# First head pair projected inside the scan's output projection, gate tiles shifted by two units

## What is computed

```python
h = rms_norm(x, g); proj = h @ w_in          # z, xbc, dt, q_a, kv_a, k_rope, gates
y_ssd = ssd_mixer(z, xbc, dt, ...) @ w_ssd_proj                # 2048 -> 1024
q  = (rms_norm(q_a) @ w_uq).reshape(16 heads, 96); kv = rms_norm(kv_a) @ w_ukv
q, k = rope(rms_norm(q)), rope(rms_norm(concat(k_nope, k_rope)))
y_mla = causal_attention(q, k, v) @ w_mla_proj
g_ssd, g_mla = split(sigmoid(gates + gate_b))
x = x + (g_ssd * y_ssd + g_mla * y_mla) @ w_o    # then a gated feed-forward part
```

## Time and profile before

| | us |
|---|---|
| median of three runs | 1760.62 (1758.84 to 1761.57) |
| the profiled execution | 1760.32 |
| its span | 1758.5 |
| TensorE, VectorE, ScalarE, GpSimd busy | 1672.8, 1079.1, 813.1, 629.1 |
| mean granted TensorE clock | 0.983 of 2.4 GHz |

### The profile page before, as it was taken

The page is one execution under the profiler, slowest core; times in us unless marked ns, Lnnn a source line. Parts: engine busy times, 40 slices in busy tenths (PEclk is TensorE's granted clock), DMA queues, the critical chain, the costliest instruction groups (busy, mean ns, idle before and its releaser), DMA issues.

```text
span 1758.5 us, 22676 instructions
## 1 busy us (share of the span) xinstructions
PE 1672.8 (95%) x7960; PEld 1316.0 (75%) x7979; DVE 1079.1 (61%) x1659; ACT 813.1 (46%) x1344; POOL 629.1 (36%) x275
## 2 busy tenths in 40 slices
PE   7999899999999799999999999999989999999999
PEld 5688677767787588766667877777768788888887
DVE  6599377666526677677778237777746555556200
ACT  5423366655334355466655235655543344444210
POOL 4244211232444144344434532222224244444442
PEclk9999899999999899999999999999999999999999
DMA  6233221121433223211112321111123233333331
GB/s 204 64 96 96 78 67 48 60 72 48 149 103 96 91 84 107 73 49 48 39 47 72 108 80 47 55 49 51 59 88 104 73 96 97 97 98 100 98 96 60
DMA packets 40119, 142.72 MB, mean 81 GB/s; under 512 B 4696, under 2 KB 5176, under 8 KB 39648
## 3 DMA queue, kind: packets, MB, share of 16 engines
q1 hardware_dynamic: 37600, 131.96, 24.6%
q10 hardware_dynamic: 2432, 9.59, 1.6%
HBM read 137.31 MB, written 4.21 MB: 80 GB/s over the span
## 4 chain that ended last, share of the span: by engine, by line
PE 78%; DVE 12%; ACT 6%; issue 3%; POOL 0%; ACTq 0%; DVEq 0%; POOLq 0%
PE bank L693 16%; PE bank L695 15%; PE bank L694 15%; PE bank L1274 4%; PE bank L1275 4%; PE bank L1273 4%; PE bank L1178 1%; PE bank L744 1%; PE bank L746 1%; PE bank L745 1%; PE bank L834 1%; PE bank L1089 1%; PE bank L1199 1%; PE bank L852 1%; PE bank L1187 1%
## 5 line engine op out<-in xcount | busy, mean ns | idle before, releaser
L584 POOL TENSOR_TENSOR w_lo<-w_raw,w_hi 128x1024 fp32r<-128x1024 f32 x243 | 591.5, 2436 | 1090.8 <-ACT w_hi L1295 946.5
L693 PE MATMUL bank<-u_hi,w_hi 128*128 128x512 f32 x776 | 326.8, 421 | 19.5 <-DVE taps L2269 10.6
L1295 ACT ACTIVATE w_hi<-w_raw 128x1024 fp32r<-128x1024 f32 x199 | 209.1, 1055 | 222.2 <-PE bank L695 177.0
L695 PE MATMUL bank<-u_hi,w_lo 128*128 128x512 f32 x776 | 305.0, 393 | 0.0
L694 PE MATMUL bank<-u_lo,w_hi 128*128 128x512 f32 x776 | 304.7, 393 | 0.0
L693 PEld LDWEIGHTS bank<-u_hi,w_hi 128*128 128x128 f32 x776 | 147.4, 190 | 78.4 <-issue 30.1
L695 PEld LDWEIGHTS bank<-u_hi,w_lo 128*128 128x128 f32 x776 | 146.8, 189 | 32.2
L694 PEld LDWEIGHTS bank<-u_lo,w_hi 128*128 128x128 f32 x776 | 147.6, 190 | 29.4 <-issue 3.4
L1273 PE MATMUL bank<-u_hi,w_hi 128*128 128x512 f32 x320 | 124.5, 389 | 0.0
L1274 PE MATMUL bank<-u_lo,w_hi 128*128 128x512 f32 x320 | 124.5, 389 | 0.0
L1275 PE MATMUL bank<-u_hi,w_lo 128*128 128x512 f32 x320 | 124.5, 389 | 0.0
(11 more groups left out here) (461 smaller groups left out, 3583.9 us busy)
## 6 DMA issues: line engine op xcount, KB each, us to landing
w_raw<-weights SPq DMA_DIRECT2D x243, 512.0 KB, 3.5
xt<-x_t SPq DMA_DIRECT2D x8, 256.0 KB, 6.6
hank<-bias_dram ACTq DMA_DIRECT2D x8, 256.0 KB, 3.1
xt<-x_t ACTq DMA_DIRECT2D x1, 2048.0 KB, 9.2
h_dram<-h_res ACTq DMA_DIRECT2D x1, 2048.0 KB, 7.0
h_res<-h_dram ACTq DMA_DIRECT2D x1, 2048.0 KB, 7.8
out<-h_res SPq DMA_DIRECT2D x8, 256.0 KB
p_val<-p_t ACTq DMA_DIRECT2D x1, 512.0 KB, 11.3
```

The costliest lines, as they stand in the source:

```text
L584: pool.tensor_tensor(w_lo[:, j, :], w_raw[:, j, :], w_hi[:, j, :].bitcast(F32), ALU.subtract).then_inc(w_lo_ready, 1)
L693: pe.matmul(o, hi, xh, start=(i == 0), stop=False)
L695: mm = pe.matmul(o, lo, xh, start=False, stop=(i == n - 1))
L1295: act.activation(w_hi[:, c % RING, :], w_raw[:, c % RING, :], ACT.Copy).then_inc(w_hi_ready, 1)
```

## The change

Seven of the eight `ssd_out` tiles turn over banks 0 and 3; the eighth lies in bank 3 and is cut into parts (0, 4), (4, 10) and (10, 16), with the keys, both queries and the sums of the first pair between. The sums of the rope part move to bank 7, and their square goes to `sq_q` ahead of ScalarE's read of the first tile. Of the first gate tile four units stand at the entry instead of eight. So in each pair a gate tile ends at steps 1 and 5 instead of 3 and 7, and the last pair has twelve units instead of eight. `key_spread` stands behind the gate units of step 4. On ScalarE the tanh comes at steps 2 and 6, the roots come ahead of the exponential of step 3, and weights are split at steps 2 and 6 instead of 0, 2 and 4. In the last pair four of the eight `o_hi` and `o_lo` are made at steps 3 to 7. `q_s`, `k_s`, `probs_x` and `turned_x` change places, and `o_hi` and `o_lo` become eight tiles each. The load of `h_res` is issued before the last sum is awaited.

```diff
@@ -147,8 +147,8 @@
-    plan.use_banks(0, 1, 2, 3)
-    plan.columns("ssd_out", 8, 16, "A")
+    plan.use_banks(0, 3)
+    plan.columns("ssd_out", 7, 16, "A")
@@ -162,23 +162,30 @@
+    plan.use_banks(3)
+    parts = [(c, s) for c in (plan.chunk(), plan.chunk()) for s in range(CH)]
+    t = plan.open("ssd_out", parts, [])
...
+    query(1, c)
+    plan.fill(t, "A")
...
-    query(1, c)
-    plan.fill(mix_gate(0, plan.chunk()), "A")
+    t = mix_gate(0, plan.chunk())
...
-        if h + 1 < XH:
+        more = h + 1 < XH
+        if more:
...
-        t = mix_gate(h, plan.chunk())
-        if h + 1 < XH:
+        gates = [plan.chunk() for _ in range(1 + more)]
+        if more:
...
+        plan.fill(t, "A")
+        if more:
...
-        plan.fill(t, "A")
-        if h + 1 < XH:
-            plan.fill(mix_gate(h + 1, plan.chunk()), "A")
+        plan.fill(mix_gate(h, gates[0]), "A")
+        if more:
+            t = mix_gate(h + 1, gates[1])
@@ -436,11 +443,11 @@
-        probs_x = at("probs_x", 56, [P, 4, S])
-        turned_x = at("turned_x", 64, [P, 4, S])
+        probs_x = at("probs_x", 186, [P, 4, S])
+        turned_x = at("turned_x", 194, [P, 4, S])
...
-        q_s = at("q_s", 186, [P, 4, S])
-        k_s = at("k_s", 194, [P, 4, S])
+        q_s = at("q_s", 56, [P, 4, S])
+        k_s = at("k_s", 64, [P, 4, S])
@@ -454,8 +461,8 @@
-        o_hi = at("o_hi", 186, [P, KD, S], F32R)
-        o_lo = at("o_lo", 104, [P, KD, S], F32R)
+        o_hi = [at(f"o_hi{i}", kb, [P, S], F32R) for i, kb in enumerate((166, 168, 202, 204, 186, 188, 190, 192))]
+        o_lo = [at(f"o_lo{i}", kb, [P, S], F32R) for i, kb in enumerate((136, 138, 140, 142, 144, 146, 148, 194))]
@@ -1100,7 +1107,7 @@
-            for i, t in enumerate(st["ssd_out"]):
+            for i, t in enumerate(st["ssd_out"][0:7]):
@@ -1128,9 +1135,8 @@
-                pe.wait_ge(act_freed, st["ssd_out"][7]["freed"][1])
...
-                    mm = pe.matmul(bank[3][:, ti:ti + 1], probs_x[NOPE:QK, 3, ti * P:(ti + 1) * P],
+                    mm = pe.matmul(bank[7][:, ti:ti + 1], sq_q[NOPE:QK, ti * P:(ti + 1) * P],
@@ -1204,26 +1210,34 @@
-            gate0 = st["mix_gate"][0]
+            gate0, last_out = st["mix_gate"][0], st["ssd_out"][7]
+            def of_y(k):
+                return y_hi[:, k, :], y_lo[:, k, :]
+            rope_sums()
...
+            column_tile(last_out, of_y, part=(0, 4))
+            project_query(1)
+            query_sums(0)
+            column_tile(last_out, of_y, part=(4, 10))
+            key_sums(0)
+            query_sums(1)
+            column_tile(last_out, of_y, part=(10, 16))
+            key_spread(0)
...
-            column_tile(gate0, of_u2, part=(0, 2))
-            rope_sums()
-            query_sums(0)
-            key_sums(0)
+            column_tile(gate0, of_u2, part=(0, 1))
...
-            project_query(1)
-            column_tile(gate0, of_u2, part=(2, 5))
-            query_sums(1)
-            column_tile(gate0, of_u2, part=(5, 7))
-            key_spread(0)
+            column_tile(gate0, of_u2, part=(1, 3))
+            pe.wait_ge(act_freed, last_out["freed"][1])
+            head_logits(0)
...
-            column_tile(gate0, of_u2, part=(7, 8))
-            for n in range(3):
-                head_logits(n)
+            head_logits(1)
+            head_logits(2)
+            column_tile(gate0, of_u2, part=(3, 4))
@@ -1233,12 +1247,13 @@
+                g, k = divmod(16 * p + 2 * i + 4, KD)
+                if more or i < 4:
+                    column_tile(st["mix_gate"][g], of_u2, part=(k, k + 2))
+                else:
+                    column_tile(st["mix_gate"][XH - 1], of_u2, part=(i, i + 1))
...
-                if more:
-                    column_tile(st["mix_gate"][2 * p + 1 + i // 4], of_u2, part=(i % 4 * 2, i % 4 * 2 + 2))
-                else:
-                    column_tile(st["mix_gate"][2 * p + 1], of_u2, part=(i, i + 1))
@@ -1251,7 +1266,7 @@
-            column_tiles(st["mla_out"], lambda k: (o_hi[:, k, :], o_lo[:, k, :]), n_lo["o"] - KD, pair=True)
+            column_tiles(st["mla_out"], lambda k: (o_hi[k][:, :], o_lo[k][:, :]), n_lo["o"] - KD, pair=True)
@@ -1724,17 +1739,19 @@
-            for i, t in enumerate(st["ssd_out"]):
-                for c, s in t["parts"][:-1]:
-                    if s == CH - 1:
-                        split_weights(c)
+            act.wait_ge(lo_ready, n_lo["kn"])
+            act.activation(sq_q[NOPE:QK, :], small2[NOPE:QK, :], ACT.Square).then_inc(krope_sq, 1)
+            def scan_out(i):
+                t = st["ssd_out"][i]
...
-            act.wait_ge(h_spilled, 16)
-            act.activation(probs_x[NOPE:QK, 3, :], small2[NOPE:QK, :], ACT.Square).then_inc(krope_sq, 1)
+            for i in range(7):
+                split_weights(st["ssd_out"][i]["parts"][0][0])
+                scan_out(i)
@@ -1788,28 +1805,29 @@
+            act.wait_ge(krope_summed, 1)
...
-            act.wait_ge(krope_sq, 1)
...
+            query_squares(1)
+            split_weights(st["ssd_out"][7]["parts"][0][0])
+            act.wait_ge(krope_added, 1)
+            head_norms(0)
+            scan_out(7)
...
-            query_squares(1)
-            after(st["head_q"][1])
-            act.wait_ge(krope_added, 1)
-            head_norms(0)
...
-            mix_gate(0)
-            after(st["mix_gate"][0])
...
-                if p and i == 0:
+                if i == 2:
...
-                if more and i == 4:
+                if more and i == 6:
...
+                if more and i == 3:
+                    head_norms(p + 1)
@@ -1817,21 +1835,19 @@
-                if more and i == 3:
-                    head_norms(p + 1)
...
-                if p and i == 0:
-                    after(st["mix_gate"][2 * p])
-                if more and i == 2:
-                    after(st["head_q"][2 * p + 3])
-                if more and i == 4:
+                if i == 2:
+                    after(st["head_q"][2 * p + 3] if more else st["mix_gate"][2 * p])
+                if more and i == 6:
...
+                if not more and 3 <= i < 7:
+                    act.wait_ge(k_ready, XH)
+                    act.activation(o_hi[i - 3][:, :], o_raw[:, i - 3, :], ACT.Copy).then_inc(hi_ready, 1)
+            act.dma_start(h_res[:, :, :].rearrange("p a b -> p (a b)"), h_dram).then_inc(h_back, 16)
+            for i in range(4, KD - 1):
+                act.activation(o_hi[i][:, :], o_raw[:, i, :], ACT.Copy).then_inc(hi_ready, 1)
...
-            act.dma_start(h_res[:, :, :].rearrange("p a b -> p (a b)"), h_dram).then_inc(h_back, 16)
-            for i in range(KD - 1):
-                act.wait_ge(x_out, i + 1)
-                act.activation(o_hi[:, i, :], o_raw[:, i, :], ACT.Copy).then_inc(hi_ready, 1)
-            act.activation(o_hi[:, KD - 1, :], bank[7][:, :], ACT.Copy).then_inc(hi_ready, 1)
+            act.activation(o_hi[KD - 1][:, :], bank[7][:, :], ACT.Copy).then_inc(hi_ready, 1)
@@ -2467,6 +2483,7 @@
+            dve.wait_ge(h_spilled, 16)
@@ -2474,22 +2491,22 @@
-            query_features(0, 0)
-            key_features(0)
-            query_features(0, 1)
...
-            values_out(0)
...
-            dve.tensor_scalar(krope_bias[:, :], bank[3][:, 0:NT], 1.0 / QK, EPS, ALU.mult, ALU.add).then_inc(krope_added, 1)
-            values_out(1)
+            dve.tensor_scalar(krope_bias[:, :], bank[7][:, 0:NT], 1.0 / QK, EPS, ALU.mult, ALU.add).then_inc(krope_added, 1)
+            query_features(0, 0)
+            key_features(0)
+            query_features(0, 1)
...
+            values_out(0)
+            values_out(1)
@@ -2519,13 +2536,15 @@
-                if i == 6 and 2 * p + 1 < KD:
+                if i == 7 and 2 * p + 1 < KD:
...
+                if not more and 4 <= i < 8:
+                    low(o_raw[:, i - 4, :], o_hi[i - 4][:, :], o_lo[i - 4][:, :])
...
+            for i in range(4, KD - 1):
+                low(o_raw[:, i, :], o_hi[i][:, :], o_lo[i][:, :])
...
-            for i in range(KD - 1):
-                low(o_raw[:, i, :], o_hi[:, i, :], o_lo[:, i, :])
-            low(bank[7][:, :], o_hi[:, KD - 1, :], o_lo[:, KD - 1, :])
+            low(bank[7][:, :], o_hi[KD - 1][:, :], o_lo[KD - 1][:, :])
```

## The result

The changed kernel takes 1776.13 us (median; 1775.17 to 1777.97), the kernel before in the same comparison 1759.74 us (1758.84 to 1761.57). The ratio is 1.0093, 95% interval 1.0076 to 1.0111: the change makes the kernel 16.4 us slower. The profiled execution has a span of 1776.2 us, 17.7 above that of before, and a mean clock of 0.977 (0.983 before).

What follows compares the result with a forecast made beforehand. TensorE, busy for 95% of the span, was taken to bound the kernel. The terms 10.3 + 2.0 - 2.7 + 4.2 - 0.5 - 4.8 = +8.5 us on 1760.32 gave 1769 us, range 1758 to 1778.

Steps and rivals of the forecast that it cites:

- rival A: The whole sum as it stands: 1769 us, own range 1764 to 1774; chance 0.55.
- rival E: A second table load at the tanh of step 6, or like collisions: 9.0 us more, 1777.8; chance 0.14.
- Part 1: Scan's output projection: TensorE waits for a bank until ScalarE reads tile 0, +10.3 us; half clock behind it, +2.0 us.
- Rival D: Banks cost nothing if ScalarE drains tile 0 before the latents: 1756.5 us, faster; chance 0.05.
- Part 2: Entry into the attention: old idle and half clock go, three new gaps and one half-clock stretch come; -2.7 us.
- three gaps: Entry waits: second query for its bank 2.0 us, second half of values 0.9, fourth logits block behind a table load 1.1.
- term of the clock: Entry: one half-clock stretch behind the first gap, chance about a half, counted as 1.5 us.
- Part 3: Seven pairs with a successor: old waits go, waits for tanh and turned_x come; +0.6 us each, +4.2 together.
- Rival B: Pairs come out even, one wait replaced by another: 1764.6 us; chance 0.18.
- Rival C: Pairs lose all waits and gain 11.8 us, the tanh off TensorE's path: 1752.8 us; chance 0.08.
- Part 4: Last pair: a wait of 0.95 goes, 0.42 comes, -0.5 us; exit: shorter wait and less half clock, -4.8 us.

Runs made afterwards that it cites:

- one part alone: Kernel before, with only the scan's eight output tiles turning over banks 0 and 3: 1771.3 us beside 1760.7, ratio 1.0063.
- banks-back version: Changed kernel, with the scan's first seven output tiles turning over banks 0, 1, 2, 3, 0, 3, 0: 1759.94 us, ratio 0.9995.
- last version: Combined version, with the tanh of each pair's odd gate tile one step earlier on ScalarE: 1747.25 us, ratio 0.9920.
- combined version: Banks-back version, with the wait for the second query filled, second weight copy two steps later, key spread ahead of step 4's gate units: 1751.9 us, ratio 0.9954.
- experiment at the exit: Banks-back version, with the four result tiles split during the last pair split behind it instead: 1762.21 us, ratio 1.0010.
- version with the copy moved: Banks-back version, with ScalarE's second weight copy of step 2 moved to step 4 in each pair: 1755.35 us, ratio 0.9973.
- changed kernel with the filled gap: Changed kernel, with seven units instead of four of the last scan tile ahead of the second head's query: 1771.99 us, ratio 1.0055.

## Why the prediction was right, and where it was not

The forecast was 1769 us, slower, in a range of 1758 to 1778; the time is 1776.13. The sign and the main mechanism were right, the size was short: 8.5 us were forecast, 16.4 measured. That the time still lies in the range is in part luck: it is above 1774, where the range of the sum itself (rival A) ended, and what stretched the range upwards was rival E, whose mechanism did not come. The same execution, step by step, from the table of starts:

**Part 1, the banks.** Forecast +10.3 and +2.0 us, measured +10.3 and +1.7. The first 7 tiles end 13.5 us later, of which 1.5 lie ahead of the wait, in stages that the change does not touch. The forecast's start of 973.8 for the waiting matmul is 975.32 with that 1.5. Shown by one part alone (10.5 us slower) and by undoing it (16.2 us faster). Rival D, that the banks cost nothing, is out.

**Part 2, the entry.** Forecast -2.7, measured about -0.2. From the end of the seventh tile to the keys of the second round it takes 2.1 us less; 2.7 of gate work have left this stretch for the last pair, and one longer pair (0.86) lies in it. The three gaps came as told: 1.88 (forecast 2.0), 0.90 (0.9), 0.92 (1.1). The step that failed is the term of the clock: I counted 1.5 us lost, and 3.2 were lost. That it comes with the bank wait I had not seen at all; I had priced both waits by themselves.

**Part 3, the pairs.** Forecast +0.6 us a pair, measured +0.86: 31.6 us from keys to keys instead of 30.75. The waits at the tanh of step 2 (listed 0.24; forecast 0.42) and for `turned_x` (0.77; 0.8) came; in the three pairs with half clock 0.46 and 0.60 for the keys take the place of the latter. In a pair at full clock four waits sum to 1.61 us, where two of 1.38 were before. The other 0.63 us are busy time (30.01 against 29.38), and the starts tell what it is. Timeline of the changed kernel, the same small matmul without and with a wait behind it:

```profile
1138.86 0.22 PE L1185 MATMUL bank<-tri_b,squares_b 128*128 128x128 bf16 x1
1138.89 0.48 PE L700 MATMUL bank<-u_hi,w_hi 128*128 128x512 f32 x1
...
1143.32 0.22 PE L1185 MATMUL bank<-tri_b,squares_b 128*128 128x128 bf16 x1
1143.78 0.50 PE L700 MATMUL bank<-u_hi,w_hi 128*128 128x512 f32 x1 [0.24 <-ACT gm L1785]
```

The next matmul starts 0.03 us later in the one case and 0.46 in the other: a wait listed with 0.24 us costs 0.43, as forecast from starts. So a listed wait is short by about 0.2 us, and four small waits cost more than two with nearly the same sum.

The step that failed in the pairs is one that the sum did not have: three of the seven have half clock in their middle, and such a pair takes 32.96 us. Keys of three rounds in the changed kernel (timeline), 32.96 and 31.63 us apart:

```profile
1100.38 0.47 PE L1131 MATMUL bank<-kn_hi,w_hi 128*128 128x512 f32 x1
...
1133.34 0.47 PE L1131 MATMUL bank<-kn_hi,w_hi 128*128 128x512 f32 x1
...
1164.97 0.47 PE L1131 MATMUL bank<-kn_hi,w_hi 128*128 128x512 f32 x1
```

That is 3 x 1.35 = 4.1 us, and with 7 x 0.86 the pairs cost 10.1 us and not 4.2. Rival B (pairs even) is half right in the runs: the banks-back version is level with the kernel before, but because the exit and the entry pay for the pairs. Rival C (pairs gain) is not what this order does, but what a better one does: with the last version the pair is at 30.29. Rival E, a second table load in each pair, is out: the changed kernel loads the table of the exponential eight times and that of the roots seven times, as before. Its sum came near the measured time by another cause.

The load's price is as I took it. In the combined version's rows the load starts at 1097.47 and the exponential that needs it at 1098.77, 1.30 us later. The Trainium skill (ScalarE: Activation LUTs, What ACT_TABLE_LOAD costs) adds a drain of about 1.38 us; no run here shows it. Its rule that tanh and the exponential share a set (Table sets: the hidden batching unit) agrees with the eight loads.

**Part 4, last pair and exit.** Forecast -0.5 and -4.8, of the latter -3.3 in the wait and -1.5 in the clock. In the last pair the first wait went from 0.78 to 0.24 us, -0.5. Measured at the exit: the wait from 5.28 to 1.54 us, -3.7, and no half clock behind it, where it had cost 2.8 (the first 12 matmuls, from start to start): -6.5. The clock's half of the term was too small. The experiment at the exit shows the same pair, a longer wait and half clock behind it.

The parts sum to 12.0 - 0.2 + 10.1 - 0.5 - 6.5 = 14.9; the other 2.8 us of the span lie in stages ahead of and behind the change (1.5 ahead of the bank wait, the rest behind the exit), where the instructions are the same and half clock falls elsewhere. My sum missed 6.4 us by three terms of the clock: +1.7 at the entry, +4.1 in the pairs, -1.3 at the exit, and by one of the pairs' length, 0.26 us each or +1.8; all the rest comes to +0.1.

**What stays open.** Why the clock falls in the middle of some pairs. In every version with the changed order of work it does so 14 to 15.5 us behind the keys of a round, in one to three rounds. In the kernel before it does not in any round's middle, although a pair there waits as long (0.50 and 0.88 us); with two banks and nothing else changed it did once, 14 us into the first round. The last version waits only 0.24 and 0.17 us a pair and still has two. The Trainium skill (TensorE: Matmul & The Clock Gate, A second HAM failure mode: psum-queue depth-cycling) tells of short idles between groups of matmuls that bring the clock down again and again; that fits the place, but it does not tell the two orders apart, as no row here does. A pair's busy time is 29.75 us in the last version and 29.38 before, with the same matmuls at full clock: most of that lies in the seams shown in part 3, since the small matmuls (`tri_b`) take 0.93 us of a pair from start to start, waits taken off, and took 0.43 before.

## What to carry to other kernels

Before banks are taken from a stage, look up when their reader really comes: here a second set of banks stood between TensorE and a reader that was 8 to 10 us late for its first tile, and no wait in the profile of before told of it. Price a wait with the clock behind it, and with the next wait behind that: two waits of 9.7 and 1.9 us, 60 us apart, cost 5.3 us more than the first alone, of which 3.2 were clock. Price waits from start to start: the length that the profile lists left out some 0.2 us each here. In a loop in which three engines hand work around, move one instruction at a time and read what is late next: spreading the keys first gained nothing alone, and with a copy and a tanh out of its way the same loop became 1.3 us a pair shorter.

## What the runs showed of the hardware that was not expected

A wait of 1.88 us was followed by half clock (6.8 us at half, 3.2 lost) in both profiles of the changed kernel, with a wait of 9.7 us some 60 us ahead, and not at all in the four profiles with the banks back, where the work between was the same; in the kernel before one of 1.96 us was, with no long wait ahead. The stretch at the exit followed waits of 5.28 and 3.61 us; behind 1.54 us there was none in eight profiles, those of the changed kernel and its copy among them, and one that cost 1.6 us in the version with the copy moved and in the changed kernel with the filled gap. And the clock fell in the midst of a loop whose waits are 0.2 to 0.9 us, at the same point of the round each time it did, and at places that an unchanged copy repeats within about 1 us once its shift of 3.4 us is taken off.
